# Triangular inverse of a recurrence by 32x32 diagonal blocks instead of 64x64, and the lanes that share TensorE in step instead of staggered

## The reference

```python
def step(state, inp):
    r_t, w_t, k_t, v_t, kk_t, a_t = inp
    sa = jnp.einsum('bhvk,bhk->bhv', state, -kk_t)
    state = (state * w_t[:, :, None, :] + sa[..., None] * (kk_t * a_t)[:, :, None, :]
             + v_t[..., None] * k_t[:, :, None, :])
    return state, jnp.einsum('bhvk,bhk->bhv', state, r_t)
```

## Time and profile before

| | before |
|---|---|
| time, median of 3 executions | 2102.4 us (2100.26 to 2102.45) |
| profiled execution: its own time | 2100.61 us |
| profiled execution: span | 2098.8 us |
| mean granted clock of TensorE over the span | 0.948 |
| PE matmuls, busy | 1863.1 us, 89% |
| DVE, ACT, POOL busy | 53%, 42%, 10% |
| stage "units", first gram product to last product of a unit | 270.1 to about 650.5 us |

### The profile page before, as it was taken

The page is one execution under the profiler, slowest core; times in us unless marked ns, Lnnn a source line. Parts: engine busy times, 40 slices in busy tenths (PEclk is TensorE's granted clock), DMA queues, the critical chain, the costliest instruction groups (busy, mean ns, idle before and its releaser), DMA issues.

```text
span 2098.8 us, 40122 instructions
## 1 busy us (share of the span) xinstructions
PE 1863.1 (89%) x16962; PEld 1558.0 (74%) x16962; DVE 1109.6 (53%) x1711; ACT 886.5 (42%) x1423; POOL 214.4 (10%) x214
## 2 busy tenths in 40 slices
PE   5899779888898889999997799799979999679996
PEld 3776568777787688888876676698877677569985
DVE  1457564565545554224344765565445574556863
ACT  2336544353431444214224256564332465346652
POOL 0000035334342000000000100010000000000210
PEclk9999889999999999999998899899989999789998
DMA  8233232222231312233323310365534534134552
GB/s 268 92 121 109 77 121 85 87 91 91 83 103 42 121 61 92 90 100 101 101 80 58 133 61 25 103 186 190 186 108 148 169 98 151 65 124 161 181 163 99
DMA packets 201377, 237.19 MB, mean 113 GB/s; under 512 B 14347, under 2 KB 158573, under 8 KB 201197
## 3 DMA queue, kind: packets, MB, share of 16 engines
q1 hardware_dynamic: 195856, 227.33, 34.2%
q10 hardware_dynamic: 5341, 7.30, 1.0%
HBM read 233.56 MB, written 1.05 MB: 112 GB/s over the span
## 4 chain that ended last, share of the span: by engine, by line
PE 75%; DVE 10%; ACT 6%; issue 2%; POOL 2%; SPq 2%; DMA 2%; ACTq 0%; DVEq 0%; POOLq 0%
PE bank L1377 17%; PE bank L1378 17%; PE bank L1379 17%; PE bank L1569 9%; ACT window L2448 2%; SPq L2896 2%; DVE window L1869 2%; PE bank L1557 2%; PE bank L1536 2%; PE bank L1548 2%; PE bank L1428 1%; PE bank L1442 1%; DVE window L1920 1%; PE bank L1754 1%; PE bank L1576 1%
## 5 line engine op out<-in xcount | busy, mean ns | idle before, releaser
L1377 PE MATMUL bank<-window 128*128 128x512 f32 (+1 forms) x2136 | 762.8, 357 | 55.1 <-DVE window L1920 29.6
L1378 PE MATMUL bank<-window 128*128 128x512 f32 (+1 forms) x2136 | 749.8, 351 | 0.0
L1379 PE MATMUL bank<-window 128*128 128x512 f32 (+1 forms) x2136 | 749.0, 351 | 0.0
L1869 DVE TENSOR_TENSOR window<-arena,window 128x2048 fp32r<-128x2048 f32 (+1 forms) x164 | 372.1, 2269 | 271.5 <-ACT window L2448 269.7
L1377 PEld LDWEIGHTS bank<-window 128*128 128x128 f32 x2136 | 415.5, 195 | 119.0 <-DVE window L1920 30.7
L2448 ACT ACTIVATE window<-arena 128x2048 fp32r<-128x2048 f32 (+3 forms) x292 | 377.1, 1291 | 211.0 <-PE bank L1379 123.5
L1379 PEld LDWEIGHTS bank<-window 128*128 128x128 f32 x2136 | 415.2, 194 | 51.3
L1378 PEld LDWEIGHTS bank<-window 128*128 128x128 f32 x2136 | 416.0, 195 | 48.2 <-issue 0.2
L2448 ACT ACTIVATE arena<-bank 128x256 f32<-128x256 f32 (+1 forms) x298 | 127.0, 426 | 367.1 <-PE bank L1379 128.6
L1569 PE MATMUL bank<-arena 64*64 64x64 f32 (+1 forms) x5888 | 215.2, 228 | 18.8 <-DVE arena L1363 10.2
L1569 PEld LDWEIGHTS bank<-arena 64*64 64x64 f32 x5888 | 201.8, 137 | 35.6 <-DVE arena L1363 11.9
(11 more groups left out here) (283 smaller groups left out, 1674.8 us busy)
## 6 DMA issues: line engine op xcount, KB each, us to landing
arena<-in_w_ff SPq DMA_DIRECT2D x64, 1024.0 KB, 5.4
arena<-in_w_ada SPq DMA_DIRECT2D x48, 1024.0 KB, 5.6
arena<-in_w_in SPq DMA_DIRECT2D x23, 1024.0 KB, 5.1
arena<-in_w_ffn_up SPq DMA_DIRECT2D x22, 1024.0 KB, 5.0
arena<-in_w_ffn_down SPq DMA_DIRECT2D x10, 1024.0 KB, 5.1
arena<-in_w_in_even SPq DMA_DIRECT2D x9, 1024.0 KB, 5.5
arena<-in_w_out SPq DMA_DIRECT2D x8, 1024.0 KB, 5.2
arena<-in_w_in_odd SPq DMA_DIRECT2D x8, 1024.0 KB, 6.9
```

What stands on the lines that cost most here:

```text
L1377: e.matmul(o, rr(l[0]), rr(r[0]), start=start, stop=False)
L1378: e.matmul(o, rr(l[0]), rr(r[1]), start=False, stop=False)
L1379: return e.matmul(o, rr(l[1]), rr(r[0]), start=False, stop=stop)
L1869: e.tensor_tensor(rr(raw), raw, rr(w.high, F32), SUB).then_inc(*ve.tick(w.ready))
```

## The change

The inverse is made in another shape. The 64x64 triangular matrix is seen as two 32x32 triangular blocks on the diagonal and one 32x32 block beside them. With two heads that gives four diagonal blocks, in partitions 0 to 31, 32 to 63, 64 to 95 and 96 to 127, and `blocks` writes a 32x32 matmul for each, in four tiles of the array. Levels 0 to 4 run on these blocks alone. Level 5 is computed as a cross product: tile q in, the other half of the same head out. `z.W` holds the inverses of the blocks, `z.TT` the full 64x64 inverse: POOL spreads the diagonal ("tt diagonal"), ACT copies the cross block into it, negated, in two copies of 32 partitions. A new step "unit blocks" makes the products for the diagonal and cross blocks alone, from operands of 64 partitions and 32 columns. POOL masks the four levels in one operation of 128x512 instead of five of 128x256. DVE's subtractions are of 128x256 instead of 128x512. The three transposes come ahead of the levels, "unit lv" behind them. The delay of 4n rounds is gone. Two small tables more are loaded, `lvl` is a third as large.

```diff
-        z.W, z.K, z.S = [spare_or_new(NCH, 2, 64) for _ in range(3)]
-        z.L = [spare_or_new(NCH, 64) for _ in range(2)]
+        z.L, z.LO, z.W = spare_or_new(NCH, 4, 32), spare_or_new(NCH, 2, 32), spare_or_new(NCH, 2, 32)
...
     def lane(n, queue):
-        for _ in range(4 * n):
-            yield
         while queue:
...
         take("gram l", *u)
+        step("unit blocks", *u)
+        give("gram l", *u)
+        yield
         take("gram r", *u)
         take("gram k", *u)
         step("unit grams", *u)
...
+        for part in "abk":
+            take("turned", *u, part)
+            step("unit turned", *u, part)
+            give("turned", *u, part)
         yield
         for l in range(1, 6):
...
+        def blocks(o, l, r, cross=False):
+            for c in range(NCH):
+                for h, b, q in QUARTERS:
+                    out = 64 * h + 32 * (1 - b) if cross else q
+                    t = e.matmul(o[out:out + 32, c], l[q:q + 32, c], r[q:q + 32, c], start=True, stop=True)
+            return t
...
+            for i, (x, y, cross) in enumerate(((a, b, 0), (b, a, 0), (b, a, 1))):
+                for c in range(NCH):
+                    for h, s, q in QUARTERS:
+                        (h0, h1), s1 = HALVES[h], s ^ cross
+                        t = e.matmul(o[q:q + 32, c, i], x[h0:h1, c, 32 * s:32 * s + 32], y[h0:h1, c, 32 * s1:32 * s1 + 32],
+                                     start=True, stop=True)
...
-            products(chunks_of(b.b, 64), z.L[l % 2], z.W[:, :, 0]).then_inc(*pe.tick(b.full, at("level read", *u)))
+            if l < 5:
+                t = blocks(o, z.L[:, :, l - 1], z.W[:, :, 0])
+            else:
+                t = blocks(o, z.LO[:, :, 1], z.W[:, :, 0], cross=True)
...
-                products(pairs_of(b.b)[:, :, 0], z.W[:, :, 1], z.X)
-            products(pairs_of(b.b)[:, :, 1], z.X, z.W[:, :, 1]).then_inc(*pe.tick(b.full))
+                o = blocks_of(b.b, 2)
+                blocks(o[:, :, 0], z.W[:, :, 1], z.X)
+                blocks(o[:, :, 1], z.X, z.W[:, :, 1]).then_inc(*pe.tick(b.full))
+            else:
+                blocks(blocks_of(b.b, 1)[:, :, 0], z.X, z.W[:, :, 1], cross=True).then_inc(*pe.tick(b.full))
```

More of the change, by code:

```diff
@@ L747, in unit @@
             give("tlt", *u, l)
[L748 to L756, removed]
             yield
+        take("lv", *u)
+        step("unit lv", *u)
+        give("lv", *u)
+        yield
         take("solved", *u)
@@ L1622, in unit_solve @@
             z, o = lane_of[u][0], bank("solved", *u)
-            pe.wait_ge(o.before, at("w", *u, 5), at("turned", *u, "a"), at("lv", *u))
-            products(pairs_of(o.b), z.W[:, :, 1], z.S).then_inc(*pe.tick(o.full))
+            pe.wait_ge(o.before, at("tt", *u), at("turned", *u, "a"), at("lv", *u))
+            products(pairs_of(o.b), z.TT, z.S).then_inc(*pe.tick(o.full))
         def unit_out(*u):
@@ L1628, in unit_out @@
             pe.wait_ge(o.before, at("solved", *u), at("r masked", *u), at("turned", *u, "b"))
[L1629 removed]
+            products(pairs_of(o.b), z.N[:, :, 0], z.G).then_inc(*pe.tick(o.full))
         def unit_states(*u):
@@ L2574, in turn_p, with unit_blocks @@
                 copy(a.PT[i % a.NT][h][0:kw, 0:nk * 128], u.b[0:kw, 0:nk * 128]).then_inc(*sc.tick(u.empty, at("pt", S, i, h)))
+        def unit_blocks(*u):
+            (z, before), g = lane_of[u], bank("gram l", *u)
+            sc.wait_ge(sc.last(), g.full, *([at("unit free", *before)] if before else stage("even")))
+            copy(z.LO, blocks_of(g.b, 3)[:, :, 1:3]).then_inc(*sc.tick(at("l", *u)))
         def unit_grams(*u):
[L2579 to L2582, removed]
+            z, gr, gk = lane_of[u][0], bank("gram r", *u), bank("gram k", *u)
             sc.wait_ge(sc.last(), gr.full)
-            copy(z.G[:, :, 1], chunks_of(gr.b, 64)).then_inc(*sc.tick(gr.empty, at("r", *u)))
+            copy(z.G[:, :, 0], chunks_of(gr.b, 64)).then_inc(*sc.tick(gr.empty, at("r", *u)))
             sc.wait_ge(sc.last(), gk.full)
@@ L2590, in unit_lt, with unit_tlt @@
             sc.wait_ge(sc.last(), b.full)
-            copy(z.X, chunks_of(b.b, 64)).then_inc(*sc.tick(b.empty, at("x", *u)))
+            copy(z.X, blocks_of(b.b, 1)[:, :, 0]).then_inc(*sc.tick(b.empty, at("x", *u)))
+        def unit_tlt(p, d, half, l):
+            z, b = lane_of[p, d, half][0], bank("tlt", p, d, half, l)
+            if l == 5:
+                for h in range(2):
+                    q = 64 * h + 32 * d
+                    sc.wait_ge(sc.last(), b.full, at("tt diagonal", p, d, half))
+                    copy(z.TT[q:q + 32, :, 32 * (1 - d):32 * (1 - d) + 32], blocks_of(b.b, 1)[q:q + 32, :, 0], scale=-1.0).then_inc(
+                        *sc.tick(*([b.empty, at("tt", p, d, half)] if h else [])))
         def unit_turned(*u):
             z, b = lane_of[u[:3]][0], bank("turned", *u)
-            o = {"a": z.S[:, :, 0], "b": z.G[:, :, 2], "k": z.B}[u[3]]
+            o = {"a": z.S[:, :, 0], "b": z.G[:, :, 1], "k": z.B}[u[3]]
             sc.wait_ge(sc.last(), b.full)
@@ L2826, in gpsimd, with unit_blocks @@
         gp.begin(e)
-        def unit_grams(*u):
[L2829 to L2834, removed]
+        def unit_blocks(*u):
+            (z, before), d = lane_of[u], u[1]
+            gp.wait_ge(gp.last(), at("recurrence consts"), at("l", *u))
+            e.tensor_tensor(z.L, z.LO[:, :, 0:1].to_broadcast([128, NCH, 4, 32]), lvl[:, d:d + 1].to_broadcast([128, NCH, 4, 32]), MUL).then_inc(
+                *gp.tick(at("levels", *u)))
+        def unit_grams(*u):
+            z, d = lane_of[u][0], u[1]
             gp.wait_ge(gp.last(), at("r", *u))
-            e.tensor_tensor(z.G[:, :, 1], z.G[:, :, 1], tri[:, d:d + 1, 1, :].to_broadcast([128, NCH, 64]), MUL).then_inc(
+            e.tensor_tensor(z.G[:, :, 0], z.G[:, :, 0], tri[:, d:d + 1, 1, :].to_broadcast([128, NCH, 64]), MUL).then_inc(
                 *gp.tick(at("r masked", *u)))
@@ L2839, in unit_grams, with unit_tlt @@
             e.tensor_tensor(z.K, z.K, tri[:, d:d + 1].to_broadcast([128, NCH, 2, 64]), MUL).then_inc(*gp.tick(at("k masked", *u)))
[L2841 to L2847, removed]
+        def unit_tlt(*u):
+            z = lane_of[u[:3]][0]
+            if u[3] == 4:
+                gp.wait_ge(gp.last(), at("w", *u))
+                e.tensor_tensor(z.TT.rearrange("p c (a t) -> p c a t", a=2), z.W[:, :, 1:2].to_broadcast([128, NCH, 2, 32]),
+                                diag2.unsqueeze(1).to_broadcast([128, NCH, 2, 32]), MUL).then_inc(*gp.tick(at("tt diagonal", *u[:3])))
         def part_o(k):
@@ L2878, in gpsimd @@
         later = lambda f: lambda p, d: f(e, gp, p, d) if p else None
-        steps = {"unit grams": unit_grams, "unit lt": unit_lt, "prep exps": later(keys), "prep scale": later(scaled), "prep last": later(rotated),
+        steps = {"unit blocks": unit_blocks, "unit grams": unit_grams, "unit tlt": unit_tlt, "prep exps": later(keys), "prep scale": later(scaled), "prep last": later(rotated),
                  "part o": part_o, "ff1": ff1, "mask bias": mask_bias, "ret gates": ret_gates, "up": up,
```

60 lines of the change are left out of this document (37 added, 23 removed).

## The result

The change made the kernel slower: median 2189.07 us (2186.04 to 2192.6) against 2101.96 us (2100.26 to 2102.45) for before, ratio 1.0416 (95% interval 1.0396 to 1.0437). The forecast was 2054, the range ended at 2108, and "slower" had 0.16.

What follows compares the result with a forecast made beforehand. PE's own work was taken to bound the stage, 324 of 380.5 us. Work -42, waits for "prepared" with clock -27, new waits +20 gave -49 us: 2054 us after rounding, range 2025 to 2108.

Steps and rivals of the forecast that it cites:

- "slower": Outcome that the change loses time: most of the fixed rate and the rest of the clock; chance 0.16.
- The price of a 32-column matmul: PE's small products in the stage: 8 ns each, 8704 matmuls in 69.6 us, 50.4 less than those replaced.
- changes of shape: PE's switches between tile shapes in the stage: 75 more at 0.11 us, costing 8.4 us.
- the waits for "prepared": PE's waits in the stage for a pair's preparation: about 8 us instead of 28; with the clock, gain 27 us.
- The rival of a fixed rate: PE takes matmuls from its queue at a fixed rate; at 25 ns 2198 us, at 16 ns 2105; chance 0.14.
- four starts in 30 ns: Argument from L1428: four matmuls begin, one in each column tile, so different tiles start about 7 ns apart.
- The clock: PE's lower clock level in the stage: loss put at 4 us instead of about 11, with fewer long waits.
- The rival "the clock": Small tiles and gaps keep the stage at 1.2 GHz for 110 us instead of 30: 2101 us; chance 0.05.
- New waits for ACT and DVE: PE's rounds in the stage get shorter; some 40 steps from ACT and DVE come late, costing 20 us.
- four tiles work side by side: 32-column matmuls on PE run in four tiles at once, following each other at about 8 ns.
- nothing outside the stage moved by over 2 us: Sign in the profile after: matters outside of the stage stay within 2 us.
- The forecast of 332 us for the stage: Sign in the profile after: the stage, 380.5 us before, should last about 332 us.

Runs made afterwards that it cites:

- e1: The change with the second head's block products left out, two tiles side by side instead of four; 2112.35 us, ratio 1.0054.
- e6: The change with the two products of unit blocks that share weights made one of 64 columns, 512 matmuls fewer; 2177.35 us, ratio 1.0358.
- e2: The change with every block product of the levels issued twice, 7168 matmuls more; 2401.88 us, ratio 1.1429.
- e5: The change with every block product of the levels streaming its 32 columns twice, same number of matmuls; 2180.11 us, ratio 1.0396.
- e7: The kernel before with 64x64 levels but the new order: transposes ahead of the levels, lv behind, no stagger; 2105.12 us, ratio 1.0003.
- e3: The change with the old delay of 4n rounds for lane n put back; 2172.9 us, ratio 1.0337.
- e9: The change with the second head's block products left out and the first head's 32 columns streamed twice; 2113.14 us, ratio 1.0065.
- e8: The kernel before with every 64x64 product of the levels issued twice, 3584 matmuls more; 2182.9 us, ratio 1.039.

## Why the prediction was wrong

**The price of a 32-column matmul** is the step that failed: "I take 8 ns". In a burst it nearly holds. After the change a level's three groups of 64 take

```profile
574.00 1.98 PE L1595 MATMUL bank<-arena 32*32 32x32 f32 x192
...
728.67 0.75 PE L1595 MATMUL bank<-arena 32*32 32x32 f32 x64
```

0.75 us for a group of 64, the upper end of the 0.6 to 0.75 foretold. By the starts in the trace, the bursts of 48 or more at the full clock run at 8.8 to 9.3 ns a matmul (29 bursts), those at the lower level at 11.9 to 14.4 (18 bursts). Sustained, the price does not hold. Put into the prediction's own sum: the stage grew by 91.3 us, of which 8.4 are changes of shape (the prediction's estimate, which no run measures) and -2.9 the waits for "prepared"; so 8704 matmuls cost 91.3 - 8.4 + 2.9 + 120.0 = 205.8 us, 23.6 ns each (all that the stops and the clock cost is in it). The runs that add or remove matmuls give 21.4 (e1), 22.9 (e6) and 29.7 (e2, no slack left). So 8 to 9 ns was the bound of the array, and 28 ns the bound of the supply, which no row of before had shown. The prediction had no term for the supply of instructions.

**The rival of a fixed rate** was right in its number: 2198 at 25 ns, with 12.9 ns (12.8 in its text) as the point from which it decides. Its mechanism was not quite it. Nothing limits one matmul to 25 ns; the limit is a block of 128 matmuls in 3.6 us. The page that I named, "TensorE: Matmul & The Clock Gate" of the Trainium skill, section "Wait — 56ns, not 53.3ns?", gives a floor of 25 ns from start to start. The bursts contradict it for different tiles (64 in 0.75 us), and the time came out near it all the same, for another reason. I argued against the rival with four starts in 30 ns. A burst of four can't speak for 8704; its groups of 16 stand between long work, where a block lasts for many microseconds.

**Why the kernel before did not show it.** Its narrow products run at 29.3 ns, so 128 of them take 3.75 us, just more than a block needs to come. PE's own pace hid the supply, with 0.9 us of stops in the stage.

**The clock** was put at 4 us of loss instead of 11; it went from 0.96 to 0.77 instead. That shows in the 40.0 us that the work besides the products is busy for longer; that the clock is the reason is borne out by e5, where all work but the level products is busy for 33.6 us less at 0.90. So the growth of 91.3 us is 75.2 us of stops instead of 0.9, some 15 us less of the other waits, 40.0 us more of other work and 6.5 less for the products (the list of waits adds up to a little more than the idle time). The rival "the clock" had the direction and too small a chance: by this account it is the second part, about half of the stops. The two can't be taken apart wholly. Stops are idle time too, and idle time went with a low clock in the earlier trace rows, but e1 with 11.7 us of stops has only 0.82; the runs that raise the clock further also add work on the array, and no run takes the stops away with all else kept.

**The waits for "prepared"**, 28 us to 8 in the forecast, stayed at 26.7. e7 shows that the new order doesn't bring them down: with it, the kernel before waits for 42.0 us. They nearly vanish (3.6 us) only where PE has much more to do ahead of them (e2), which is no gain. One reading behind this term was off: of POOL's seven operations from lora to "prepared", six take 1.26 to 1.30 us, and L1345 takes 0.61.

**New waits for ACT and DVE**, 20 us in the sum, are nearly absent: 2.0 us for ACT at L1439 and under 1 us for DVE at L1595. With PE slower than planned both are always ahead of it.

**Right:** four tiles work side by side, at about 9 ns in a burst, and nothing outside the stage moved by over 2 us. The forecast of 332 us for the stage missed by 141: 75.2 of issue stops, 51.4 for the small products (121.0 of busy time instead of 69.6), 18.7 of waits for "prepared" that didn't go, less some 17 of new waits that didn't come. The remaining 12 or so are not measured apart; the rest of the work at the lower clock is in them, less other waits that went.

No version tried beats the kernel before. The nearest to it in the change's own direction, e6 and e3, recover 12 and 16 of 87 us.

## What to carry to other kernels

Before cutting matmuls into smaller tiles, count them: PE here got 128 float32 matmuls of the trace, with their weight loads, every 3.6 us or so where it was starved, and in no run in under 3.26, so a stream that is faster than 28 ns for a pair holds for a block or two and then stops. Compare the number of transfers on the instruction queue with the time of the stage (65 in 381 us had room, 100 in 473 had not where they came in a row), and prefer fewer matmuls with more columns: here doubling the columns left the time as it was, and doubling the matmuls cost 213 us. A price read from a short burst is a bound, not a rate.

## What the runs showed of the hardware

- Blocks of 16,384 bytes of instructions for PE came 3.6 us apart in starved stretches, also with a DMA share of 0.02 (e2). The profile doesn't name it: PE's idle time says "issue", stops of 1 to 5 us, in the middle of a group. That the recording of the trace has no part in the 3.6 us is not shown by any run.
- The granted clock depends on more than stops: 0.82 with 32 columns and 0.90 with 64 in the same number of matmuls and few stops (e1, e9), 0.98 with 64x64 tiles (e8), 0.77 and 0.83 for the same matmuls in step and staggered, with nearly the same stops (after, e3).
- Four 32x32 tiles side by side take a float32 matmul of the trace every 9 ns in a burst at the full clock and every 13 ns or so at the lower level.
